# Sample attention of a hybrid decoder step: three small products with the narrow operand as TensorE's weight, in four column groups, and their results turned on TensorE

## The reference

```
q_lat = einsum('nthd,chd->nthc', q[..., :QK_NOPE], w_uk)      # latent queries
s = (q_lat . ckv + q_pe . kr) * ATTN_SCALE;  p = softmax(s)
o_lat = einsum('nhts,nsc->nthc', p, ckv)                      # output in the latent space
o = einsum('nthc,chd->nthd', o_lat, w_uv)                     # value products
m = o @ w_o
```

## Time and profile before

| what | value |
|---|---|
| median of 3 runs | 1463.28 us (1462.86 to 1465.5) |
| span of the profiled execution | 1461.2 us |
| TensorE busy | 1409.3 us (96%) |
| VectorE, ScalarE, POOL busy | 894.1 us (61%), 536.8 us (37%), 175.0 us (12%) |
| mean granted clock of TensorE | 0.985 |

### The profile page before, as it was taken

One profiled execution on the slowest core, in us unless ns is written; L12 is line 12 of the kernel. 1 busy time (PEld: TensorE's weight loads), 2 busy tenths in 40 slices (PEclk: granted clock), 3 DMA queues, 4 the chain that ended last, 5 costly groups with the idle time before them and its releaser, 6 DMA issues.

```text
span 1461.2 us, 30495 instructions
## 1 busy us (share of the span) xinstructions
PE 1409.3 (96%) x11815; PEld 1329.9 (91%) x11815; DVE 894.1 (61%) x1518; ACT 536.8 (37%) x870; POOL 175.0 (12%) x329
## 2 busy tenths in 40 slices
PE   6999999998999999999999989998999999999997
PEld 5999999998999999999989855657999999999997
DVE  4444664227888888633375686464578888884334
ACT  4545443236222223333464212344543222223334
POOL 1000000000222222100001020100012322321000
PEclk9999999999999999999999999799999999999999
DMA  7332222321332232233425463101223233222331
GB/s 232 103 86 73 73 75 82 91 87 48 97 100 87 86 100 80 78 96 89 119 69 187 176 248 125 48 1 34 83 60 100 86 94 92 86 77 88 92 90 65
DMA packets 224370, 138.20 MB, mean 95 GB/s; under 512 B 12620, under 2 KB 220674, under 8 KB 223256
## 3 DMA queue, kind: packets, MB, share of 16 engines
q1 hardware_dynamic: 219688, 112.38, 26.5%
q0 software_dynamic: 4224, 24.62, 4.5%
q10 hardware_dynamic: 384, 0.16, 0.1%
HBM read 133.83 MB, written 3.67 MB: 94 GB/s over the span
## 4 chain that ended last, share of the span: by engine, by line
PE 91%; DVE 5%; ACT 2%; issue 1%; DMA 1%; SPq 0%; DVEq 0%; ACTq 0%
PE psum L659 76%; PE psum L1054 2%; PE psum L1183 1%; PE psum L1160 1%; PE psum L1037 1%; PE psum L718 1%; PE psum L1015 1%; PE psum L818 1%; PE psum L1163 1%; DVE ut L1686 1%; DVE x L1689 1%; DVE kt L1978 1%; DMA xn<-in_x_prompt 1%; PE psum L1172 1%; DVE wl L1647 1%
## 5 line engine op out<-in xcount | busy, mean ns | idle before, releaser
L1647 DVE TENSOR_TENSOR wl<-ws,wh 128x1024 fp32r<-128x1024 f32 x217 | 265.8, 1225 | 336.5 <-ACT wh L1243 173.5
L659 PE MATMUL psum<-xh,wh 128*128 128x260 f32 x2064 | 426.6, 285 | 11.0 <-DVE xl L1666 6.2
L659 PE MATMUL psum<-xh,wl 128*128 128x260 f32 x2064 | 421.5, 283 | 0.0
L659 PE MATMUL psum<-xl,wh 128*128 128x260 f32 x2064 | 420.6, 283 | 0.0
L659 PEld LDWEIGHTS psum<-xh,wh 128*128 128x128 f32 x2064 | 320.9, 189 | 14.3 <-issue 13.5
L659 PEld LDWEIGHTS psum<-xh,wl 128*128 128x128 f32 x2064 | 320.6, 189 | 0.0
L659 PEld LDWEIGHTS psum<-xl,wh 128*128 128x128 f32 x2064 | 320.0, 188 | 0.4
L1243 ACT ACTIVATE wh<-ws 128x1024 fp32r<-128x1024 f32 x144 | 152.2, 1057 | 319.1 <-PE psum L659 319.1
L659 PE MATMUL psum<-acth,wh 128*128 128x260 f32 x704 | 144.3, 284 | 0.0
L659 PE MATMUL psum<-acth,wl 128*128 128x260 f32 x704 | 143.2, 282 | 0.0
L659 PE MATMUL psum<-actl,wh 128*128 128x260 f32 x704 | 143.0, 282 | 0.0
(11 more groups left out here) (283 smaller groups left out, 1812.9 us busy)
## 6 DMA issues: line engine op xcount, KB each, us to landing
ws<-in_w_up SPq DMA_DIRECT2D x88, 512.0 KB, 3.8
ws<-in_w_in_a SPq DMA_DIRECT2D x32, 512.0 KB, 4.1
ws<-in_w_down SPq DMA_DIRECT2D x32, 384.0 KB, 3.4
ws<-in_w_down SPq DMA_DIRECT2D x32, 320.0 KB, 3.1
ws<-in_w_out_a SPq DMA_DIRECT2D x16, 512.0 KB, 3.9
ws<-in_w_o SPq DMA_DIRECT2D x8, 512.0 KB, 4.6
xn<-in_x_prompt SPq DMA_DIRECT2D x4, 512.0 KB, 10.1
ws<-in_w_dq SPq DMA_DIRECT2D x4, 512.0 KB, 4.6
```

The source lines that it names most:

```text
L659: mm = pe.matmul(psum[:, 2 * slot + b, 0:HB], w, r[:, k, b * HB:(b + 1) * HB], start=st, stop=en)
L1647: dve.tensor_tensor(low_, ws[:, slot4, :], f32(high), ALU.subtract).then_inc(w_low, 1)
```

## The change

The narrow operand becomes the weight, and the wide one moves. Latent queries: 32 columns of `qn` (the last 24 of the prompt and the 8 samples) are the weight and the 256 columns of a head's `ukt` move, four heads side by side in four column groups, 8 products instead of 16. Merged outputs: 32 columns of `fr` (8 and 24 cleared ones) are the weight, 256 columns of `osb` move, 8 products instead of 16. Value products: 32 columns of `olT` (8 and 24 cleared ones) and 128 moving ones of `uv`, 16 products as before. The results then lie with samples on the partitions; ScalarE copies each bank to `turn` in SBUF and TensorE turns it by transposes (4, 4 and 2). Around this, expansions 14 and 15 and the row blocks are put between the steps, VectorE's half of clearing `qz` goes to POOL, four of VectorE's eight copies into `qz` go to ScalarE, the turn of `so` goes behind the first score chunk of sample 1, and waits for `os_ready` and for the five row blocks move a little further down TensorE's queue.

```diff
@@ -266,3 +266,3 @@
             ("wdg", [NS, H], F32), ("so64", [NS, H], F32), ("so", [H], F32), ("sown", [NS], F32), ("wp4", [GRP, NS], F32), ("wpr", [NS], F32),
-            ("fr", [NS, H], F32))
+            ("fr", [NS, 32], F32))
         ukt = at("ukt", [H, CL], lat2_end + size([KC, T]) + size([T]))
@@ -274,2 +274,5 @@
         assert pt_end <= arena
+        turn = at("turn", [2 * CL], tmp_base)
         lat = [at(f"lat{i}", [KPP, CL], base) for i, base in enumerate((arena, arena + slot, cqr_base, arena + 2 * slot))]
@@ -294,3 +297,3 @@
             arena + slot, ("o", [H, T], F32), ("ppt0", [4, SEQ], F32), ("ppt1", [4, SEQ], F32), ("ownp", [KC, NS, H], F32),
-            ("olT", [KC, H, NS], F32))
+            ("olT", [KC, H, 32], F32))
         assert ok_end <= arena + 2 * slot + size([KPP, CL])
...
@@ -398,2 +403,6 @@
             return 2 * (g // 8) + g % 2, (g % 8) // 2
+        def turned_latents(rows):
+            return psum[rows, 0, :].rearrange("p (c h e) -> p c h e", c=KC, e=32)[:, :, :, 32 - NS:]
@@ -618,2 +627,4 @@
             pool.wait_ge(mm_done, U_UQ + 6)
+            pool.wait_ge(w_low, U_O)
+            pool.memset(qz[:, 0:QB // 2, :, :], 0.0).then_inc(qz_clear, 1)
             pool.wait_ge(rotq_step, 8)
@@ -1059,6 +1070,6 @@
             pe.wait_ge(evac_uq, 12)
-            for c in range(KC):
-                for h in range(H):
-                    mm = pe.matmul(psum[:, 0, (c * H + h) * NS:(c * H + h + 1) * NS], ukt[:, h, c * P:(c + 1) * P], qn[:, h, SEQ:T],
-                                   start=True, stop=True)
+            for r in range(2):
+                for g in range(GRP):
+                    h = GRP * r + g
+                    mm = pe.matmul(psum[32 * g:32 * g + 32, 2, r * CL:(r + 1) * CL], qn[:, h, T - 32:T], ukt[:, h, :], start=True, stop=True)
             mm.then_inc(ql_done, 1)
@@ -1072,2 +1083,12 @@
             mm.then_inc(qsel_done, 1)
+            def turn_narrow(bank):
+                for c in range(KC):
+                    for r in range(2):
+                        mm = pe.transpose(psum[:, bank, (2 * c + r) * P:(2 * c + r + 1) * P], turn[:, r * CL + c * P:r * CL + (c + 1) * P], ident)
+                return mm
+            pe.wait_ge(ql_read, 1)
+            turn_narrow(0).then_inc(qlT_done, 1)
             for g in range(2):
@@ -1075,3 +1096,4 @@
-            pe.wait_ge(qown_ready, 3)
+            pe.wait_ge(own_low, 1)
+            pe.wait_ge(qown_ready, 2)
             pe.wait_ge(ckt_ready, KC)
@@ -1087,5 +1109,2 @@
-            pe.wait_ge(so_ready, 2)
-            pe.transpose(psum[0:H, 3, 0:NS], so[0:NS, :], ident[0:NS, 0:NS]).then_inc(sn_done, 1)
-            pe.wait_ge(sn_ready, 1)
             for s in range(NS):
@@ -1093,2 +1112,5 @@
                     score(s + 1, 0)
+                if s == 0:
+                    pe.wait_ge(so_ready, 2)
+                    pe.transpose(psum[0:H, 3, CL:CL + NS], so[0:NS, :], ident[0:NS, 0:NS]).then_inc(sn_done, 1)
                 expand(s + 2 if s < 6 else 2 * s - 4)
@@ -1097,2 +1119,4 @@
                     score(s + 1, 1)
+                if s == 0:
+                    pe.wait_ge(sn_ready, 1)
                 weigh(s)
@@ -1117,7 +1141,11 @@
             pe.wait_ge(osn_ready, NS)
-            for c in range(KC):
-                for s in range(NS):
-                    mm = pe.matmul(psum[:, 1, (c * NS + s) * H:(c * NS + s + 1) * H], osb[:, s, c * P:(c + 1) * P], fr[:, s, :],
-                                   start=True, stop=True)
+            for r in range(2):
+                for g in range(GRP):
+                    s = GRP * r + g
+                    mm = pe.matmul(psum[32 * g:32 * g + 32, 1, r * CL:(r + 1) * CL], fr[:, s, :], osb[:, s, :], start=True, stop=True)
             mm.then_inc(olp_done, 1)
+            expand(14)
+            pe.wait_ge(ols_ready, 1)
+            turn_narrow(2).then_inc(olpT_done, 1)
@@ -1137,3 +1165,3 @@
-            for c in range(5):
+            for c in range(2):
                 new_rows(c)
@@ -1141,14 +1169,18 @@
             pe.wait_ge(olT_ready, 1)
-            for h in range(H):
+            for r in range(2):
                 for c in range(KC):
-                    mm = pe.matmul(psum[:, 0, h * NS:(h + 1) * NS], uv[:, c, h * P:(h + 1) * P], olT[:, c, h, :],
-                                   start=(c == 0), stop=(c == KC - 1))
+                    for g in range(GRP):
+                        h = GRP * r + g
+                        mm = pe.matmul(psum[32 * g:32 * g + 32, 3, r * P:(r + 1) * P], olT[:, c, h, :], uv[:, c, h * P:(h + 1) * P],
+                                       start=(c == 0), stop=(c == KC - 1))
             mm.then_inc(os_done, 1)
-            for g in range(14, 16):
-                expand(g)
-            pe.wait_ge(os_ready, 1)
-            pe.wait_ge(n_ready, 5)
+            for c in range(2, 4):
+                new_rows(c)
+            pe.wait_ge(oss_ready, 1)
+            for r in range(2):
+                mm = pe.transpose(psum[:, 3, CL + r * P:CL + (r + 1) * P], turn[:, r * P:(r + 1) * P], ident)
+            mm.then_inc(osT_done, 1)
+            expand(15)
+            new_rows(4)
...
@@ -1519,10 +1555,13 @@
             act.activation(qz[:, QB // 2:, :, :].rearrange("p a b c -> p (a b c)"), cst[:, 0:half_qz], ACT.Copy, scale=0.0).then_inc(qz_clear, 1)
+            act.wait_ge(ql_done, 1)
+            act.activation(turn[:, :], psum[:, 2, :], ACT.Copy).then_inc(ql_read, 1)
             act.wait_ge(qz_clear, 2)
-            act.wait_ge(ql_done, 1)
-            act.activation(qown[64:, 0:2, :].rearrange("p c (s h) -> p c s h", s=NS), psum[64:, 0, 0:2 * H * NS].rearrange("p (c h s) -> p c s h", c=2, h=H),
+            act.wait_ge(qlT_done, 1)
+            act.activation(qown[64:, 0:2, :].rearrange("p c (s h) -> p c s h", s=NS), turned_latents(slice(64, P)).rearrange("p c h s -> p c s h"),
                            ACT.Copy).then_inc(qown_ready, 1)
-            for i in range(4):
-                for j in range(2, 4):
-                    mm = act.activation(latent_rows(i, j), psum[32 * j:32 * j + 32, 0, 0:2 * H * NS].rearrange("p (c h s) -> p c s h", c=2, h=H),
-                                        ACT.Copy)
+            for j in (2, 3, 1):
+                if j == 1:
+                    act.wait_ge(own_low, 1)
+                for i in range(4):
+                    mm = act.activation(latent_rows(i, j), turned_latents(slice(32 * j, 32 * j + 32)).rearrange("p c h s -> p c s h"), ACT.Copy)
             mm.then_inc(qz_a, 1)
@@ -1556,5 +1595,2 @@
                 act.wait_ge(pv_done, s + 1)
-                if s == 0:
-                    act.wait_ge(ql_done, 1)
                 act.activation(osb[:, s, :], psum[:, 3, 0:CL], ACT.Copy).then_inc(osn_ready, 1)
@@ -1584,7 +1620,14 @@
             expanded(13)
+            act.wait_ge(olp_done, 1)
+            act.activation(turn[:, :], psum[:, 1, :], ACT.Copy).then_inc(ols_ready, 1)
             split(U_O, U_O % STAGES, U_O % 2, staged(U_O))
+            for c in range(2):
+                new_rows(c)
+            act.wait_ge(os_done, 1)
+            act.activation(turn[:, 0:CL], psum[:, 3, 0:CL], ACT.Copy).then_inc(oss_ready, 1)
+            for c in range(2, 4):
+                new_rows(c)
             split(U_O + 1, (U_O + 1) % STAGES, (U_O + 1) % 2, staged(U_O + 1))
-            for c in range(5):
-                new_rows(c)
             expanded(15)
+            new_rows(4)
@@ -1981,5 +2024,4 @@
             dve.wait_ge(mm_done, U_O)
-            dve.memset(qz[:, 0:QB // 2, :, :], 0.0).then_inc(qz_clear, 1)
             dve.memset(mxa[:, :], 0.0).then_inc(mx_step, 1)
-            for c in range(3):
+            for c in range(2):
                 turn_keys(0, c)
@@ -1987,8 +2029,8 @@
+            dve.wait_ge(qlT_done, 1)
+            dve.tensor_copy(qown[0:64, 0:2, :].rearrange("p c (s h) -> p c s h", s=NS),
+                            turned_latents(slice(0, 64)).rearrange("p c h s -> p c s h")).then_inc(own_low, 1)
             dve.wait_ge(qz_clear, 2)
-            dve.wait_ge(ql_done, 1)
-            dve.tensor_copy(qown[0:64, 0:2, :].rearrange("p c (s h) -> p c s h", s=NS), psum[0:64, 0, 0:2 * H * NS].rearrange("p (c h s) -> p c s h", c=2, h=H)).then_inc(qown_ready, 1)
             for i in range(4):
-                for j in range(2):
-                    mm = dve.tensor_copy(latent_rows(i, j), psum[32 * j:32 * j + 32, 0, 0:2 * H * NS].rearrange("p (c h s) -> p c s h", c=2, h=H))
+                mm = dve.tensor_copy(latent_rows(i, 0), turned_latents(slice(0, 32)).rearrange("p c h s -> p c s h"))
             mm.then_inc(qz_v, 1)
...
@@ -2040,2 +2082,3 @@
+            dve.memset(fr[:, :, :], 0.0).then_inc(narrow_clear, 1)
             dve.wait_ge(e_done, NS)
...
@@ -2076,3 +2120,4 @@
             dve.wait_ge(merge, 14)
-            dve.tensor_tensor(fr[:, :, :], wpr[:, :].rearrange("p (s o) -> p s o", o=1).to_broadcast([P, NS, H]),
+            dve.wait_ge(narrow_clear, 1)
```

(14 more changed lines are left out.)

11 lines of the change are left out of this document (9 added, 2 removed).

## The result

The changed kernel takes 1454.54 us (median of 4 runs, 1453.61 to 1454.8), the kernel before 1464.05 beside it; the ratio is 0.993, with a 95% interval of 0.9917 to 0.9942. So it gained about 9.5 us where 16.3 were forecast, and it lies 1.5 us above the range. The profiled span is 1453.0 us against 1461.2, 8.2 less. Times and ratios here leave out six executions of 2291 to 7704 us (four of the kernel before, one each of e3 and e14).

What follows compares the result with a forecast made beforehand. TensorE, holding 91% of the chain that ended last, was taken as the bound. First place 5.6 plus second place 10.7 gave 16.3 us: span 1461.2 to 1444.9, median 1447.0 us, range 1443.8 to 1453.0.

Steps and rivals of the forecast that it cites:

- Beside this ScalarE does ... from 830.75, to 835.1: First place: ScalarE's copies take 4.35 us from 830.75, so scores of sample 0 start at 835.2 instead of 838.35.
- I take 5.6, about two thirds of the way from the low case: First place: gain put at 5.6 us, between 3.95 (clock falls) and 6.35 (full clock holds).
- the low case: First place: the clock falls in the scores of sample 0 as now, 2.4 us are lost and 3.95 stay.
- for a later landing I take 0.5 us off: 10.7: Second place: third pair of prompt scores 11.2 us sooner, less 0.5 for row copies landing later, 10.7.
- TensorE's part: Second place: TensorE starts at 911.52 and reaches the first prompt scores at 920.65 instead of 932.64.
- The third rival: Second place: row copies land late and ScalarE holds everything behind block 3; with 5 us, 1452; chance 0.07.
- the 13.2 of the forecast: Second place: forecast time from the place's start to the third pair of prompt scores, 13.2 us.
- The prediction's own sign: Second place: the prediction is wrong if ScalarE waits for the row copies beyond 920.
- the wait for the turned bank: First place: TensorE waits some 0.3 us for ScalarE's copy of the first bank, ahead of the transposes.
- rival 4: Both places: the column groups do not run side by side; 8.8 us back, 1455.8; chance 0.03.
- rival 5: First place: POOL's memset is too slow to hide; at 54 us the kernel takes 1498 us; chance 0.03.
- the second rival: Second place: transposes are no activity for the clock, first scores run at half; 1.5 us lost, 1448.5; chance 0.05.

Runs made afterwards that it cites:

- e3: The changed kernel with POOL's last three gathers of the first four samples and the value weights' load held back until the turned latent queries are copied; 1455.01 us, ratio 0.9926.
- e14: The changed kernel with only the rope rows' gathers for samples 4 to 7, the latent rows of samples 0 to 3 used again; ratio 0.9897.
- e9: The kernel before, unchanged, run once more for a second profile; 1464.92 us in one execution.
- e10: The changed kernel, unchanged, run once more for a second profile; 1459.9 us in one execution.
- e2: The changed kernel with two more buffers for the new rows, so row blocks 3 and 4 don't wait for transfers of blocks 1 and 2; 1450.24 us, ratio 0.9885.
- e1: The changed kernel with the second place (merged outputs, value products, row order, splits) put back as before, leaving the latent queries' half; ratio 0.9973.
- e5: The kernel before with only the second place changed (merged outputs, value products, row and split order); ratio 0.996.
- e7: The changed kernel with four buffers for the new rows and both the first gathers and the loop's gathers held back; 1448.1 us, ratio 0.9898.
- e15: The changed kernel with four buffers for the new rows and the first gathers held back, the loop's gathers where they were; 1450.8 us, ratio 0.9905.

## Why the prediction was wrong

The stretches below come from TensorE's timelines: from the first latent-query product to the expansion of sample 2, from there to the first merged-output product, from there to the third pair of prompt scores, and from there to the end.

```
                    start   first   loop   second    rest     span
before, as read    828.47   16.66   66.39   23.88   525.80   1461.2
before again (e9)  827.91   18.19   69.48   22.56   524.26   1462.4
after              828.27   15.09   69.19   14.63   525.82   1453.0
after again (e10)  830.56   15.10   69.31   14.35   527.48   1456.8
four rows (e2)     830.20   14.97   67.66   11.81   523.86   1448.5
```

Against the profile that I read the change gains 1.57, -2.80 and 9.25 us; against the second one 3.10, 0.29 and 7.93. The second account fits e1 and e5 better, where the first place gives 1.9 to 5.9 us and the second 4.2 to 7.6 by the intervals: 3.10 + 0.29 lies inside, and 7.93 just above, or inside with the 1.56 us that the rest took more.

**The first place, "Beside this ScalarE does ... from 830.75, to 835.1": this step failed.** The chain of copies took the 4.35 us that I worked out (4.34 measured), but began at 833.22, because TensorE's signal was held 2.4 us while POOL issued indirect gathers (828.77 to 832.22) and a load (to 833.00). e3, e7 and e15 show it by its removal. Nothing of before warned of it: there the products themselves ended at 832.2, when the gathers were through (831.3). The prediction also put at nothing what POOL's memset does to the gathers behind it; it moved them from 827.86 to 828.77, into the forecast copies, and no run takes that part by itself.

**"I take 5.6, about two thirds of the way from the low case": it came out low.** The clock fell in the scores of sample 0, as in the low case, in both profiles of the changed kernel (3.37 and 3.43 us for the next expansion); in ten other kernels with the new first place it fell three times and held seven. Seven of twelve is near the two thirds that the prediction took; that both profiles of the changed kernel fell is a draw, for 1.4 us.

**The loop was taken as unchanged from one profile.** It is unchanged (69.48 and 69.19), but the profile had 66.39. This is no error of the sum, but the reason why the two spans seem to show a loss of 2.8 us in code that the change does not touch.

**The second place, "for a later landing I take 0.5 us off: 10.7": this step failed.** TensorE's part was right (8.95 against 9.13 us). The way from the copy of block 0 to that of block 3, 3.84 us in the earlier trace rows, took 6.13 (916.80 to 922.93). The third rival named this mechanism and priced it at 5 us; its size was 2.3, plus the clock that TensorE lost by waiting (2.04 and 2.04 us instead of 1.56 and 1.88; of nine profiles with this wait only e3's kept the clock). It is shown by e2: without the wait the third pair comes at 11.81 us, 2.82 sooner than in the changed kernel and 1.4 us sooner even than the 13.2 of the forecast. The prediction's own sign came too, ScalarE waiting for the row copies beyond 920. The 2.3 us lie in the landing, not in POOL's issues: the `kr` stores of the row blocks land after 3.7 us (median) in the changed kernel and 3.6 and 3.4 in e2, with 512 KB of `w_o` loading beside them from 918 on, and after 1.8 in before, e9 and e1, with no load there. That the load does it I have not tested apart.

**The base of that term, 23.88 us, was 1.3 us too long**, and that of the first place 1.5 too short, as e9 shows. The terms put together, against the second profile: first place and loop 5.6 + 1.5 (base) - 2.4 (held signal) - 1.4 (clock) = 3.3, measured 3.10 + 0.29; second place 10.7 - 1.3 (base) - 1.5 (landing) = 7.9, measured 7.93, which agrees by construction, since base and landing are the measured differences; the rest took 1.56 us more, of which 0.5 are the third pair's own products (2.04 us instead of 1.56 at full clock) and the remainder varies as much over all profiles, whose code behind the third pair is the same (522.4 to 528.9 us). With the start that makes the 9.4 us by which the spans differ; between e9 and e10 it is 5.6. The split rests on single profiles; that the held signal is worth its whole 2.4 us isn't shown, since e3 won back 1.0 of it and lost the rest to the next held signals.

**Right:** the products at 1.07, 1.07 and 1.08 us; the wait for the turned bank (0.42 us for 0.3); the column groups side by side (rival 4); POOL's memset, 1.17 us where I took 1.5, hidden (rival 5); and the clock through the transposes: 1.00 from 905 to 924, with 21 transposes among the work. The page "TensorE: Matmul & The Clock Gate", Part 4, of the Trainium skill would not count them as busy; the second rival that came of it (first scores at half clock) did not appear in any profile here, though other products stand between the transposes. The kernel's end shows them alone: in the changed kernel TensorE runs nothing but transposes of `x` from 1438.29 on, with waits between them, and the granted clock is 0.50 from 1441 to 1446.5 and 1.00 again from 1447.5 to 1449. It comes back like this in all 17 profiles, which the page's rule would not give.

## What to carry to other kernels

When an operation becomes short, look at what its old length covered: here the slow products had ended at 832.2, when the gathers' issue was through (831.3), and the fast ones put a signal that others wait for into its middle. Moving the gathers (e3) only put them over the next signals. A wait for a buffer that cost nothing becomes the next bound once the engine ahead of it is fast; two more buffers took the ratio from 0.993 to 0.9885, each beside the kernel before in its own group. And take two profiles of the kernel before where a term of the sum is a microsecond or two: three stretches of the one read here differed from the next by 1.5, 3.1 and 1.3 us, while the spans differed by 1.2.
